# Scattering expert rows with an adding DMA into rows filled with zeros, in a one-core hybrid decoder step

## What is computed

```
def hier_moe(h, w_rg, b_rg, w_re, b_re, w_gate, w_up, w_down):
    ...
    y = jnp.zeros((n, D_MODEL), jnp.float32)
    for e in range(N_EXPERTS):
        hid = jax.nn.silu(t @ w_gate[e]) * (t @ w_up[e])
        y = y + combine[:, e:e + 1] * (hid @ w_down[e]).astype(jnp.float32)
    return y.astype(h.dtype).reshape(shape)
```

## Time and profile before

| what | value |
|---|---|
| time, median of 3 runs | 715.99 us (715.69 to 718.16) |
| the profiled execution | 715.4 us, of which the span is 713.7 us |
| PE busy | 692.3 us, 97% of the span |
| VectorE busy | 555.3 us, 78% |
| ScalarE busy | 451.4 us, 63% |
| GpSimd busy | 152.3 us, 21% |
| DMA packets and bytes | 80922 packets, 181.10 MB |

### The profile page before, as it was taken

How to read it: one execution, slowest core, us unless ns; L and a number is a source line. 1 busy time by engine, 2 the same in 40 slices (tenths; PEclk the granted TensorE clock), 3 DMA queues, 4 the chain that set the end, 5 groups by cost and what they waited for, 6 DMA issues and landing times.

```text
span 713.7 us, 11899 instructions
## 1 busy us (share of the span) xinstructions
PE 692.3 (97%) x3816; PEld 540.9 (76%) x3816; DVE 555.3 (78%) x890; ACT 451.4 (63%) x714; POOL 152.3 (21%) x157
## 2 busy tenths in 40 slices
PE   7999999999999999999988999999999999999995
PEld 4777777887778778777777888888888888888842
DVE  4775866866858875363887999999999999999857
ACT  7645354453465643122245888898889888898745
POOL 1010010110110131000014233333333333341114
PEclk9999999999999999999999999999999999999998
DMA  9993830330311626635339999999999999998758
GB/s 350 267 308 96 196 89 0 88 88 0 88 59 68 237 96 235 261 128 187 112 137 353 415 415 412 411 392 388 403 392 381 380 393 393 366 404 339 268 197 357
DMA packets 80922, 181.10 MB, mean 254 GB/s; under 512 B 41720, under 2 KB 45984, under 8 KB 72696
## 3 DMA queue, kind: packets, MB, share of 16 engines
q1 hardware_dynamic: 71384, 163.12, 63.0%
q0 software_dynamic: 9216, 16.93, 6.3%
q10 hardware_dynamic: 288, 0.62, 0.3%
HBM read 162.89 MB, written 34.39 MB: 276 GB/s over the span
## 4 chain that ended last, share of the span: by engine, by line
PE 85%; DVE 4%; DMA 4%; ACT 2%; issue 2%; SPq 1%; POOL 1%; DVEq 0%; ACTq 0%; POOLq 0%
PE psZ L1391 24%; PE psZ L901 20%; PE psS L1418 12%; PE psZ L1092 10%; PE psT L831 6%; PE psOG L831 2%; PE psOG L974 2%; PE psS L942 2%; DMA wo_in<-w_out 1%; PE psOG L1223 1%; PE psOG L983 1%; DMA yy<-y_d 1%; PE psOG L873 1%; DVE x1a L2692 1%; PE psT L1181 1%
## 5 line engine op out<-in xcount | busy, mean ns | idle before, releaser
L2388 DVE TENSOR_TENSOR wg_lo<-wg,wg_hi 128x1024 fp32r<-128x1024 f32 x128 | 150.7, 1218 | 2.0 <-ACT wg_hi L1531 2.0
L1531 ACT ACTIVATE wg_hi<-wg 128x1024 fp32r<-128x1024 f32 x128 | 128.8, 1062 | 3.6 <-DVE small L2550 1.6
L1391 PE MATMUL psZ<-wg_hi,xg_hi 128*128 128x512 f32 x252 | 101.4, 402 | 0.0
L1391 PE MATMUL psZ<-wg_hi,xg_lo 128*128 128x512 f32 x252 | 99.0, 393 | 0.0
L1391 PE MATMUL psZ<-wg_lo,xg_hi 128*128 128x512 f32 x252 | 99.0, 393 | 0.0
L901 PE MATMUL psZ<-wi_hi,xT_hi 128*128 128x512 f32 (+1 forms) x240 | 90.0, 375 | 1.0 <-DVE wi_lo L1963 1.0
L2774 POOL DMA_INDIRECT y_d<-y_t,idx_dst x32 | 48.9, 1528 | 188.5 <-ACT y_t L1531 188.5
L2577 DVE TENSOR_TENSOR wd_lo<-wd,wd_hi 128x2048 fp32r<-128x2048 f32 x31 | 71.1, 2292 | 21.0 <-ACT wd_hi L1531 21.0
L901 PE MATMUL psZ<-wi_lo,xT_hi 128*128 128x512 f32 (+1 forms) x240 | 87.2, 364 | 0.0
L901 PE MATMUL psZ<-wi_hi,xT_lo 128*128 128x512 f32 (+1 forms) x240 | 87.2, 363 | 0.0
L2770 POOL DMA_INDIRECT xg<-h_d,idx_src x32 | 58.5, 1830 | 22.2 <-issue 13.7
(11 more groups left out here) (354 smaller groups left out, 1346.3 us busy)
## 6 DMA issues: line engine op xcount, KB each, us to landing
wg<-w_gate SPq DMA_DIRECT2D x32, 1024.0 KB, 9.9
wg<-w_up SPq DMA_DIRECT2D x32, 1024.0 KB, 17.4
wd<-w_down SPq DMA_DIRECT2D x32, 1024.0 KB, 13.1
y_d<-wo_stage SPq DMA_DIRECT2D x1, 4608.0 KB
wi_raw<-w_in SPq DMA_DIRECT2D x4, 1024.0 KB, 14.1
x_t<-x_rows SPq DMA_DIRECT2D x8, 512.0 KB, 4.0
mix_d<-mix_t SPq DMA_DIRECT2D x8, 512.0 KB, 3.0
m_t<-mix_d SPq DMA_DIRECT2D x8, 512.0 KB, 3.7
```

The lines of the kernel that those rows point to most:

```text
L1391: last = nc.tensor.matmul(psZ[z][:], a[:, c, :], w, start=(n == 0), stop=(n == 3 * DC - 1))
L1531: return nc.scalar.activation(out, in_, ACT.Copy)
L2388: tt(wg_lo[k][:, :, c, :], wg[k][:, :, c, :], wg_hi[p][:].bitcast(F32), ALU.subtract).then_inc(s_wgl, 1)
```

## The change

Two lines differ. The indirect store adds each row to what `y_d` holds, in place of overwriting it; and the zero fill covers both rows of each pair, 2304 rows of 4 KB in place of 1152 (9216 KB in place of 4608 KB), since each row now has to hold zero before its addition. Number and order of the instructions, the semaphores and their counts stay.

```
--- before.py
+++ after.py
@@ -615,7 +615,7 @@
 
             stage1(0)
             sp.wait_ge(s_zx, 1)
-            sp.dma_start(y_d.rearrange("(t p k) n -> p t k n", p=P, k=2)[:, :, 0], wo_stage[0][:, 0:D].unsqueeze(1).to_broadcast([P, T, D]))\
+            sp.dma_start(y_d.rearrange("(t p) n -> p t n", p=P), wo_stage[0][:, 0:D].unsqueeze(1).to_broadcast([P, 2 * T, D]))\
                 .then_inc(s_zy, 16)
             sp.wait_ge(s_zs, N_WI + 2)
             for n, (c0, c1) in enumerate(WI_COLS):
@@ -2772,7 +2772,7 @@
 
             def scatter(k, rows_, done):
                 nc.gpsimd.indirect_dma_start(y_d, bass.IndirectOffsetOnAxis(rows_.bitcast(U32), 0), y_t[k][:], None,
-                                             bounds_check=pairs_end, oob_is_err=False).then_inc(done, 16)
+                                             bounds_check=pairs_end, oob_is_err=False, compute_op=ALU.add).then_inc(done, 16)
 
             def gather4(e):
                 if e >= 4:
```

## The result

The changed kernel takes 755.95 us (median of 4 runs, 755.38 to 760.16) against 717.08 us (715.69 to 718.43) for the kernel before in the same set: a ratio of 1.0548, with a 95% interval of 1.0511 to 1.0586. The profiled execution has a span of 753.6 us, 39.9 us more than before. The forecast was 745 us, in a range from 724 to 776.

The account below looks back on a forecast made before the run. PE sets the pace, with the DMA engines having nothing left over in the expert stage. Profiled 715.4 + 7.5 (fill) + 2.5 (clock) + 18.2 (addition) + 1.0 (tail) = 744.6, given as 745 us; range 724 to 776.

Parts of the forecast that it names:

- a dear addition: Rival, expert stage: a row costs three times a copy, stage gains 37.7 us, total 765; chance 0.20 (756 to 780).
- The longer fill: Stage 1: 4.72 MB more zeros ahead of the z_d stores stop PE for 7.5 us, between 0 and 11.2.
- 2.7 us of room: Stage 1: stores landed by about 49, ScalarE's pT copy waiting for them went at 51.68.
- the last step: Stage 1: VectorE's pT copy ends at about 60.6, PE's product starts at about 60.9 in place of 53.36.
- x of the next tile stays covered: Stage 1: next tile's x lands at about 68, VectorE wants it at 70.7, covered by 2 to 3 us.
- The clock: Stage 1, after the stop: PE's clock falls to 1.2 GHz and slows the first matmuls; 2.5 us, between 0 and 5.8.
- The addition: Expert stage: 28 adding scatters at 0.70 us more each delay the last up load 19.7 us; stage ends 18.2 us later.
- The step that decided the case: Expert stage: an addition costs the DMA engines one more pass, 0.70 us per scatter; chance 0.50 (734 to 756).
- 1.5 of room: End of expert stage: idle bits of ScalarE's round and a little before PE starves, together 1.5 us.
- The scatter's own path: Expert stage: doubled GpSimd issue and 2 to 4 us more landing fit in 8 us left; costs nothing.
- The tail: End of program: the last scatter, alone on the chain, costs its addition's latency; 1 us, between 0 and 3.2.
- a second trip: Tail: upper bound for the last scatter's added latency, another trip of the same kind, 3.2 us.

Follow-up runs that it names:

- the fill moved: Against the kernel before: scatter adds, the second rows' zeros a DMA of their own issued behind the next tile's loads, on another semaphore; 755.45 us, ratio 1.0525.

## Why the prediction was right, and by how much its terms were off

**Direction and mechanism.** Two prices that add up was right: 13.3 us with the fill alone, and 28.7 us with the addition and the second rows' zeros in the gap, together 42.0 against the 39.9 of the changed kernel. The forecast gave 29.2 us in four terms, the trace shows 39.9. No term was over and all were under, so nothing cancelled; the range held the result because it reached far into the case of a dear addition.

**The longer fill: 7.5 us forecast, 9.8 measured.** The term was under-sized. I had 11.2 us of writes, less 2.7 us of room, less 1 us because both copies start at once and PE's product then follows sooner. The writes and the last step came out: the writes ran at 418 to 430 GB/s until about 60, and PE's product followed ScalarE's copy by 0.5 us in place of 1.7. The room was wrong. I had read from the fall of the rate at 49 in the earlier trace rows that the stores had landed, but a landing is the semaphore and not the last byte: by the semaphore events in the traces, `s_zy` was complete at 51.47 us before the change and at 62.53 after it, 11.1 us later. ScalarE's copy went at 51.68 before the change, so the room was 0.2 us and not 2.7. It is not SP's held-up issue that made the difference: the last store was issued by 56.2, and the fill's last rows were still being written until 60.9. That x of the next tile stays covered came out: its loads went out at 62.09 and VectorE was late itself.

**The clock: 2.5 us forecast, 2.6 measured.** The matmuls after the stop started 0.43 us apart in place of 0.23, until 68.6 (10 x 0.2 = 2.0), and the product with pT, the first of these and the last cost 0.6 more. That the number is so near is luck, since it was picked between 0 and 5.8. It fell sooner than the end of the program had suggested, about 2 us and not 4 after the last work; with the fill alone it fell 4.2 us after it, at the same stop, and cost 2.1 us. The Trainium skill, page "TensorE: Matmul & The Clock Gate", part 1, describes the two levels and a fall when PE is idle; this trace agrees on both (0.50 and 1.00 granted). Another 1.1 us were lost up to the first gate product (13.5 less 9.8 and 2.6), seen first at about 250 us; I did not follow them up.

**The addition: 18.2 us forecast, 19.9 measured.** The step that decided the case was right, and its price a little low: queue 0 went from 45.0 to 70.8 us of 16 engines (9.4% of 753.6), 25.8 us for 32 scatters, 0.81 us each and not 0.70. The other kernels with additions and all gathers give 0.79 to 0.86 by the same sum. 28 of them are 22.6 us, less 1.5 of room 21.1. The doubled plain scatter put 23.1 us on the queue, 0.72 each, so an addition is one more pass and a tenth. The page "Collectives: The Full Stack" of the Trainium skill, section "The bandwidth ceiling: the fold count and why AG ≠ RS ≠ AR", with its two reads for each reduced piece, gives the same order; with a factor of (22.5 + 25.8) / 22.5 = 2.15 for the scatters, the measurement lies somewhat over its 1.93. That the time of the DMA work is what is short was shown from three sides: a plain scatter costs nearly the same (18.7 us), half the additions cost about half (9.5), and fewer gathered bytes bring the cost to nothing. SP's rounds came out at 10.2 us on average (forecast 10.1), but not as forecast in their course: eight of 9.4 to 9.6 us and then 19 of 10.5.

The stage holds a term that I had put at nothing without a reason, a fall of the clock. 3.4 us at half the clock are up to 1.7 us of PE's time, an estimate. With additions for all experts the stage grew by 19.9, 22.0 and 23.3 us in three kernels, with one, one and two such falls, and by 20.3 with additions for 28 experts and no fall. So 19.9 is one draw out of 20 to 23.

One reading under this was weaker than I took it. I argued from a DMA share of 1.00; but with hardly any gathers the share was 1.02 and PE lost nothing. The share says that there is a queue, not that it is too long. What carried the argument was the landing times, 17.0 growing to 21.1 us against 21.05 us of room. Nor did the share fall because the last weights had been issued, as I put it: it is 0.91 from 640 us on, and SP issued the last down load at 652.09. And the engines are not always short of time after the change: PE's stops hold back the next loads, and in the stretch from 560 to 600 us the rate falls for some 2 us to under 175 GB/s.

**The scatter's own path: nothing forecast.** Its issue on GpSimd rose from 1.54 to 2.2 us. Its landing, by the semaphore events of the traces, went from 8.6 to 9.9 us in the median over all 32, less than the 2 to 4 us more that I had put, and no one waited for it in the middle of the stage. Right, except at the end.

**The tail: 1.0 us forecast, 6.5 measured.** The worst term. I had put 1 us on the last landing, where the bound of a second trip was 3.2; it took 3.0 (3.23 to 6.25). I had not seen that ScalarE's last copy waits for the scatter two experts earlier, which takes 9.17 us from its issue at this point, against 6.2 before: the copy waits 3.5 us for it, and the last scatter starts 1.6 us later (6.6 us from the start of line 1409 in place of 5.0). The rows loaded after it came late enough for PE to stand for 3.6 us and lose its clock once more (0.50 from 738.0 to 741.4), which makes 1.4 of the 1.9 us that remain. With the last four scatters overwriting, the tail is within 0.5 us of before.

## What to carry to other kernels

A DMA that adds isn't free, however few its rows: it costs the DMA engines one more pass (here 0.81 us for 64.5 rows of 4 KB), and where weight loads already land as late as they may by the end of a stage, nearly each such microsecond ends up in the time, even if the first rounds don't show it. Read the room as landing time against first use, not as the DMA share, and take the landing from the semaphore, not from the moment at which the rate falls (2.5 us apart here). A bulk fill belongs in a gap, and not ahead of small transfers: it holds back the semaphores and the loads behind it, and the engine that issues. The same zeros in a gap cost under 1 us.

## What the runs showed of the hardware that was not expected

SP stands still while it issues behind a large fill. Behind 1152 rows of 4 KB the seven small stores took 0.7 to 1.7 us each to issue; behind 2304 rows one took 13.3 us, and with the order turned round the two loads behind the fill took 11.1 and 10.3 us. The issue of the fill itself takes 0.43 us in both.

The granted clock fell about 2 us after PE's last work in stage 1 of the changed kernel, 4.2 us after it at the same stop with the fill alone, and about 4 us after it at the end of the program before. It came back 5.8 us after PE had resumed, and 4.6 with the fill alone. In the expert stage it fell to 0.50 for 3.4 us at a time behind stops of only 1.2 to 2.1 us: once in the changed kernel, twice with the fill moved, once each with the doubled scatter, with the zeros in the gap and with every second expert adding. In the kernel before it did not fall there.

The second read of an addition shows in no count: queue 0 has 9216 packets before and after, and 16.93 and 16.94 MB, and the page's bytes read from memory stay at 162.89 MB; only the queue's time grows.
